# An SSD, attention and expert-retrieval block on one core: eight dense tokens fetched as gathered rows, and the v stage with v stationary

## The reference

```python
x = x + concat([y_ssd, y_diff]) @ w_out              # the mixer, 512 tokens of 1024
q  = (xb @ w_q).reshape(tb, 8, 2, 128)
sc = einsum('thjd,hjnd->thjn', q, sub_keys)          # 2 x 128 scores per head
s_half, i_half = top_k(sc, 16)
top_s, top_pos = top_k(s_half[0][:, None] + s_half[1][None, :], 16)
idx = i_half[0] * 128 + i_half[1]                    # at top_pos
g = softmax(top_s)
h = gelu(einsum('td,thkd->thk', xb, u[idx]))         # u, v: 16384 x 1024
out = einsum('thk,thkd->td', g * h, v[idx])
```

## Time and profile before

| | |
|---|---|
| median of 3 runs | 1391.71 us (1390.98 to 1391.97) |
| the profiled execution | 1390.36 us |
| its span, first to last instruction | 1388.6 us |
| granted clock of PE | 1.000 |
| PE, DVE, ACT, POOL busy | 98%, 78%, 32%, 47% of the span |
| moved by DMA | 467.69 MB, mean 337 GB/s |

### The profile page before, as it was taken

One profiled execution on the slowest core, in us unless ns is written; L12 is line 12 of the kernel. 1 busy time (PEld: TensorE's weight loads), 2 busy tenths in 40 slices (PEclk: granted clock), 3 DMA queues, 4 the chain that ended last, 5 costly groups with the idle time before them and its releaser, 6 DMA issues.

```text
span 1388.6 us, 16311 instructions
## 1 busy us (share of the span) xinstructions
PE 1364.4 (98%) x5402; PEld 934.3 (67%) x5402; DVE 1082.4 (78%) x2469; ACT 440.1 (32%) x1219; POOL 647.5 (47%) x516
## 2 busy tenths in 40 slices
PE   7999999999999999999999999999999999999999
PEld 5656648566588888888899999995444444444443
DVE  4535445899899999999998899997977677766655
ACT  2533532444412111112787887881000000000000
POOL 0000000823855443433486756774777666645430
PEclk9999999999999999999999999999999999999999
DMA  8322234975999999988799999999999999999997
GB/s 330 137 108 97 117 143 175 375 291 204 412 412 403 399 336 376 324 316 305 289 409 409 405 399 392 382 390 380 363 410 409 409 409 409 410 409 409 410 409 301
DMA packets 121763, 467.69 MB, mean 337 GB/s; under 512 B 13776, under 2 KB 14160, under 8 KB 115152
## 3 DMA queue, kind: packets, MB, share of 16 engines
q0 software_dynamic: 73728, 268.47, 49.7%
q1 hardware_dynamic: 47664, 197.66, 36.7%
q10 hardware_dynamic: 288, 0.52, 0.1%
HBM read 462.67 MB, written 3.93 MB: 336 GB/s over the span
## 4 chain that ended last, share of the span: by engine, by line
PE 71%; DVE 22%; issue 4%; ACT 1%; DMA 0%; SPq 0%; DVEq 0%; ACTq 0%
PE BANKS L953 32%; PE BANKS L929 15%; PE BANKS L729 11%; DVE X L1623 5%; PE BANKS L721 5%; PE BANKS L948 4%; DVE BIG L1434 2%; DVE BIG L1426 2%; DVE UV L1618 1%; DVE BIG L1618 1%; DVE BIG L1428 1%; DVE SMALL L1431 1%; DVE BIG L1449 1%; DVE SMALL L1423 1%; PE BANKS L701 1%
## 5 line engine op out<-in xcount | busy, mean ns | idle before, releaser
L1665 POOL DMA_INDIRECT UV<-u,IDX x173 | 217.6, 1258 | 376.6 <-DVE IDX L1495 244.4
L1665 POOL DMA_INDIRECT UV<-v,IDX x178 | 232.0, 1303 | 161.3 <-DVE X L1623 107.7
L1623 DVE SCALAR_TENSOR_TENSOR X<-UV,HG,X 128x1024 f32<-128x1024 f32 x178 | 228.4, 1283 | 33.9 <-DMA UV<-v,IDX 31.6
L1618 DVE SCALAR_TENSOR_TENSOR UV<-UV,Y 128x1024 f32<-128x1024 f32 x173 | 210.0, 1222 | 34.5 <-DMA UV<-u,IDX 34.0
L929 PE MATMUL BANKS<-T 128*128 128x256 f32 x1024 | 229.1, 379 | 0.0
L953 PE MATMUL BANKS<-T,BIG 128*128 128x512 f32 x512 | 225.2, 593 | 0.0
L953 PE MATMUL BANKS<-Y,BIG 128*128 128x512 f32 x512 | 225.1, 592 | 0.0
L929 PE MATMUL BANKS<-T,Y 128*128 128x256 f32 x992 | 221.9, 379 | 0.0
L929 PEld LDWEIGHTS BANKS<-T 128*128 128x128 f32 x1024 | 192.3, 190 | 24.5
L929 PEld LDWEIGHTS BANKS<-T,Y 128*128 128x128 f32 x992 | 186.3, 190 | 23.8
L953 PEld LDWEIGHTS BANKS<-Y,BIG 128*128 128x128 f32 x512 | 97.5, 190 | 122.3 <-issue 122.3
(11 more groups left out here) (272 smaller groups left out, 1244.7 us busy)
## 6 DMA issues: line engine op xcount, KB each, us to landing
T<-u_t SPq DMA_DIRECT2D x64, 512.0 KB, 6.7
T<-v SPq DMA_DIRECT2D x64, 512.0 KB, 6.8
Y<-v SPq DMA_DIRECT2D x64, 512.0 KB, 6.8
Y<-u_t SPq DMA_DIRECT2D x62, 512.0 KB, 6.6
BIG<-w_in SPq DMA_DIRECT2D x23, 1024.0 KB, 7.0
BIG<-w_q SPq DMA_DIRECT2D x16, 1024.0 KB, 8.9
BIG<-w_out SPq DMA_DIRECT2D x8, 1024.0 KB, 6.9
UV<-v,IDX POOLq DMA_INDIRECT x178, 9.0
```

The source lines that it names most:

```text
L1618: stt(row, row, 1.0, Y[:, n // 4, :], ALU.mult, ALU.mult, accum_out=acc).then_inc(used, 1)
L1623: stt(xb, row, HG[:, n % 2, i % UNIT:i % UNIT + 1], xb, ALU.mult, ALU.add).then_inc(used, 1)
L1665: pool.indirect_dma_start(row_place(s), None, u if kind == "ru" else v, bass.IndirectOffsetOnAxis(IDX[:, b, c:c + 1], 0)).then_inc(row_in[ ...
```

## The change

Eight of the 256 dense tokens (the first eight of block 2) are taken out of the dense part, which is now `TD` = 248 tokens wide. Their 8 x 128 = 1024 pairs of token and slot are laid out as 8 slots deep on 128 partitions (16 groups of slots by 8 tokens), so that they are done by 8 fetches of u (`mu` steps) and 8 of v (`mv`), 16 more row fetches in the same stream. Small DMAs through DRAM turn indices and weights round (`MIDX`, `MW`), ScalarE and PE copy the eight tokens to all partitions once (`my`), and `XMA` is summed back by eight small products with a selection matrix.

HBUF is 248 columns a tile, there are 62 one-hot groups in place of 64, and the v stage is turned round: pieces of v are stationary and the 248 token columns of HBUF move. The result is columns by tokens, so at the end ScalarE copies each of four banks to `OT` and PE transposes it back. `RING` goes from 8 to 7, and the buffer `YM` is new. The hand-written order of the mixer stays.

```diff
-RING = 8
+RING = 7
-NGRP = HT // NTOK
+XM = 8
+MG = P // XM
+TD = HT - XM
+NGRP = TD // NTOK
+LASTV = 3
@@ row_stream
+        m = q - LATE * UNIT - 4
+        if 0 <= m < 2 * XM and m % 2 == 0:
+            s.append(("mu", m // 2))
...
+        if 0 <= m - 2 * XM - 8 < XM:
+            s.append(("mv", m - 2 * XM - 8))
@@ work_order
-            work += [item] + rows(4 - (n >= 13))
+            work += [item] + rows(4 - (n >= 11))
...
-    work += [first] + on("sel", 0) + rows(9) + on("oh", 0) + [second] + rows(3) + on("oh", 1) + [keys, columns]
+    work += [first] + on("sel", 0) + rows(8) + on("oh", 0) + [second] + rows(3) + on("oh", 1) + [keys, columns]
...
-        while w < len(work) and spent < 3.44 * (j + 1):
+        while w < len(work) and spent < 3.35 * (j + 1):
@@ SyncE
+                if j == 46:
+                    sp.wait_ge(mi_ready, 1)
+                    sp.dma_start(m_index, MB[:, :]).then_inc(m_away, 16)
+                    sp.dma_start(m_weight, G[0:XM, HB, :]).then_inc(m_away, 16)
+                if j == 48:
+                    sp.wait_ge(m_away, 32)
+                    sp.dma_start(MIDX[:, :], m_index.rearrange("t (g k) -> g t k", k=XM)).then_inc(m_in, 16)
...
@@ TensorE, gl
-                        last = nc.tensor.matmul(PS[(i + 2) % 4][:, 0:HT], ub[:, c, :], T8[:, 1, c, :],
+                        last = nc.tensor.matmul(PS[(i + 2) % 4][:, 0:TD], ub[:, c, :], T8[:, 1, c, XM:HT],
@@ TensorE, the v stage
-                return nc.tensor.matmul(PS[4 + 2 * t + n][:, :], HBUF[:, j, t * P:(t + 1) * P],
-                                        STREAM[j % NS][:, n * HALF:(n + 1) * HALF], start=(j == 0),
-                                        stop=(j == NKEY - 1), skip_group_check=True)
+            def v_chunk(j, c):
+                at = c % 2 * HT
+                return nc.tensor.matmul(PS[4 + c // 2][:, at + XM:at + HT], STREAM[j % NS][:, c * P:(c + 1) * P],
+                                        HBUF[:, j, :], start=(j == 0 and c % 2 == 0), stop=(j == NKEY - 1), skip_group_check=True)
+            def back_to_tokens(bank):
+                pe.wait_ge(ot_done, bank + 1)
+                for c in (2 * bank, 2 * bank + 1):
+                    for b in range(HB):
+                        last = nc.tensor.transpose(PS[2 * b + c // 4][:, c % 4 * P:(c % 4 + 1) * P],
+                                                   OT[:, c, b * P:(b + 1) * P], IDENT)
+                last.then_inc(ot_full, 1)
...
+            pe.wait_ge(used, ROWSEQ[("mv", XM - 1)] + 1)
+            for c in range(KC):
+                at = c % 2 * HT
+                nc.tensor.matmul(PS[4 + c // 2][:, at:at + XM], XMA[:, c * P:(c + 1) * P], COLS[:, V_SEL:V_SEL + XM],
+                                 start=False, stop=True, skip_group_check=True)
+            for bank in range(4):
+                for c in (2 * bank, 2 * bank + 1):
+                    for j in range(NKEY - LASTV, NKEY):
+                        last = v_chunk(j, c)
+                last.then_inc(acc_full, 1)
+                if bank:
+                    back_to_tokens(bank - 1)
+            back_to_tokens(3)
@@ VectorE
+                    if step == "mu":
+                        stt(row, row, 1.0, YM[:, :], ALU.mult, ALU.mult, accum_out=MH[:, i:i + 1]).then_inc(used, 1)
+                    elif i == 0:
+                        ts(XMA[:, :], row, MHG[:, 0:1], None, ALU.mult).then_inc(used, 1)
+                    else:
+                        dve.wait_ge(used, ROWSEQ[("mv", i - 1)] + 1)
+                        stt(XMA[:, :], row, MHG[:, i:i + 1], XMA[:, :], ALU.mult, ALU.add).then_inc(used, 1)
@@ VectorE, fin
-                    for n in range(2):
-                        dve.wait_ge(acc_full, 2 * i + n + 1)
-                        xb = X[:, HB + i, n * HALF:(n + 1) * HALF]
-                        tt(xb, xb, PS[4 + 2 * i + n][:, :], ALU.add).then_inc(out_ready, 1)
+                    dve.wait_ge(ot_full, 2 * i + 2)
+                    for b in range(HB):
+                        xb = X[:, HB + b, i * HALF:(i + 1) * HALF]
+                        tt(xb, xb, PS[2 * b + i][:, :], ALU.add).then_inc(out_ready, 1)
```

More of the change, by code:

```diff
@@ L101, in work_order @@
     place = [0]
+    known = [LATE]
     def rows(m):
         out = []
-        while place[0] < len(stream) and (m or stream[place[0]][0] not in ("ru", "rv")):
+        while place[0] < len(stream) and (m or stream[place[0]][0] not in ROW_KINDS):
             item = stream[place[0]]
-            m -= item[0] in ("ru", "rv")
+            if item[0] == "ru" and item[1] >= known[0] * UNIT:
+                break
+            m -= item[0] in ROW_KINDS
             out.append(item)
@@ L225, in work_order @@
         o += rows(1 + (k % 4 == 0))
-    o += on("gm", NGRP - 1) + on("gw", NKEY - 1)
+    o += [("gm", n) for n in range(NGRP) if ("gm", n) not in o] + on("gw", NKEY - 1)
     first, second, keys, columns = pick(LATE)
@@ L428, in block_program @@
         POS = {s: i for i, s in enumerate(ORDER)}
-        rows_until = lambda step: sum(s[0] in ("ru", "rv") for s in ORDER[:POS[step]])
-        FIRST_V = rows_until(("gm", NGRP - 1))
+        rows_until = lambda step: sum(s[0] in ROW_KINDS for s in ORDER[:POS[step]])
+        FIRST_V = rows_until(("gw", NKEY - 1))
         def spaces():
@@ L971, in _ @@
-            pe.wait_ge(ge_done, NKEY)
-            pe.wait_ge(gw_done, len(WEIGHED))
-            for j in range(3, NKEY - 2):
+            for j in range(NKEY - LASTV):
+                if j == 3:
+                    pe.wait_ge(ge_done, NKEY)
+                    pe.wait_ge(gw_done, len(WEIGHED))
                 pe.wait_ge(v_in[j % NS], 16 * (j // NS + 1))
-                for t in range(HB):
-                    last = v_products(j, t)
+                for c in range(KC):
+                    last = v_chunk(j, c)
@@ L986, in _ @@
+            for j in range(NKEY - LASTV, NKEY):
+                pe.wait_ge(v_in[j % NS], 16 * (j // NS + 1))
+            for bank in range(4):
+                for c in (2 * bank, 2 * bank + 1):
+                    for j in range(NKEY - LASTV, NKEY):
+                        last = v_chunk(j, c)
+                last.then_inc(acc_full, 1)
+                if bank:
+                    back_to_tokens(bank - 1)
+            back_to_tokens(3)
         @block.scalar
@@ L1193, in _ @@
                         last = nc.scalar.activation(bank[:, 0:n], bank[:, 0:n], ACT.Gelu)
-                    if n < HT:
-                        last = nc.scalar.activation(HBUF[:, i, n:HT], bank[:, n:HT], ACT.Gelu)
+                    if n < TD:
+                        last = nc.scalar.activation(HBUF[:, i, n:TD], bank[:, n:TD], ACT.Gelu)
                     last.then_inc(ge_done, 1)
+                elif step == "my" and i == 0:
+                    nc.scalar.activation(YM[:, :].rearrange("p (c g t) -> p c g t", c=KC, g=MG),
+                                         bc(T8[:, 1, :, 0:XM], 2, MG), ACT.Copy).then_inc(my_full, 1)
+                elif step == "my":
+                    for c in range(2):
+                        act.wait_ge(my_full, c + 2)
+                        nc.scalar.activation(YM[:, c * HALF:(c + 1) * HALF], PS[5 + c][:, :], ACT.Copy).then_inc(ym_done, 1)
+                elif step == "mhg":
+                    act.wait_ge(mh_ready, 1)
+                    nc.scalar.activation(MHG[:, :], MHG[:, :], ACT.Gelu).then_inc(mhg_done, 1)
                 elif step == "gm" and JS[i] < NKEY:
@@ L1231, in _ @@
                     last.then_inc(oh_ja, 1)
+            act.wait_ge(chosen, CHOSEN[("r", 2 * PH - 1)] + 1)
+            for bank in range(4):
+                act.wait_ge(acc_full, bank + 1)
+                nc.scalar.activation(OT[:, 2 * bank:2 * bank + 2, :].rearrange("p c t -> p (c t)"), PS[4 + bank][:, :], ACT.Copy)\
+                    .then_inc(ot_done, 1)
             for n in range(2):
-                act.wait_ge(out_ready, 3 + n)
+                act.wait_ge(out_ready, HB * n + 2)
                 part = slice(n * HALF, (n + 1) * HALF)
```

110 lines of the change are left out of this document (74 added, 36 removed).

## The result

| | before | with the change |
|---|---|---|
| median | 1391.35 us (1390.98 to 1391.97) | 1399.01 us (1398.77 to 1400.64) |
| the profiled execution, its span | 1390.36, 1388.6 us | 1398.77, 1397.0 us |

The ratio is 1.0057, with a 95% interval of 1.004 to 1.0074: slower by 7.7 us. The forecast was 1403.

What follows compares the result with a forecast made beforehand. Prediction: DMA engines carrying gathered rows bound the kernel, nearly level with PE. Last row at 932.2 + 452.4 + 6.4 = 1391.0; rv, additions and store give 1399.9, 11.3 above 1388.6, so 1391.7 + 11.3 = 1403 us, range 1394 to 1411.

Steps and rivals of the forecast that it cites:

- u stage ends: End of the u stage: 945.8 us less 6.0 in its first half and 7.6 in its second, so 932.2.
- PE's end: After the v stage and the final transposes, PE alone would end near 1369.4 us.
- The rival by which PE sets it: At the kernel's end: PE decides if 185 MB pass in 433 us, 427 GB/s; 1376 us, chance 0.07.
- The rate: DMA transfers after the u stage: 409 GB/s as the ceiling when saturated, so 185.0 MB take 452.4 us.
- what would show it: Signs in the changed profile; wrong if saturated DMA exceeds 415 GB/s, rows finish before PE, or PE idles in the u stage.
- The tail: Kernel's end: the last rv steps, each behind the one before, add 2.5 us, between 0 and 3.
- theory 1: From the experiments: the bytes the DMA engines must move set when the last row is used, and with it the end.
- The hole: First choice of indices in the v stage: of 8.4 us unused transfer time, some 2 us are given back.
- The smaller ring: Row steps on VectorE: fewer ring places delay the mixer by 3 to 10 us, 1406 to 1413; chance 0.04.
- VectorE in the second half of the u stage: VectorE cannot keep up there with 7 ring places; without any gain +7.6, 1410 us; chance 0.08.
- Narrow columns: Products with narrow moving operands cost more a column, v stage 29 us more, 1403 to 1408 us; chance 0.03.
- The extra rows: Part of them hidden in better filled holes and faster running rows: 1391 to 1395 us; chance 0.06.

Runs made afterwards that it cites:

- the pair with 13 us more: Useless PE products added in the v stage: 13.0 us to the changed kernel, 1398.94 us; 12.9 us to the kernel before, 1403.91 us.
- The run with two sums and six rows less: Changed kernel, additional row every third tile in the u stage's second half, last 32 rv steps alternating between two sums: 1388.96 us, ratio 0.9983.
- the run with half of v: Changed kernel fetching only columns 0 to 511 of each v tile, all products still made: 1370.70 us, ratio 0.9853.

## Why the prediction was right, and where its numbers were off

The direction and the cause were right: the rows' bytes, not PE, decide when VectorE gets its last rows, and PE's gain is lost behind them. The sum ended 2.9 us too high (span 1399.9 forecast, 1397.0 measured). That it is no further off is partly luck, since errors of both signs cancel: the DMA engines were done 7.1 us earlier than forecast, and what follows them took 4.2 us longer. The forecast of 1403 was 4 us too high because it also added 3.1 us to the span, where these runs have 2.0.

| term of the prediction | forecast | measured |
|---|---|---|
| u stage ends | 932.2 | 932.35 |
| bytes from there to the last row | 185.0 MB | 185.9 MB |
| their time at the full rate | 452.4 us (409) | 447.0 us (416) |
| time not used in holes | 6.4 us | 4.5 us |
| DMA engines done | 1391.0 | 1383.9 |
| from there to the end of the last rv | 3.8 us | 7.2 us |
| four additions and store | 5.1 us | 5.9 us |
| PE's end | 1369.4 | 1369.5 |

The bytes are 412 x 424.15 + 409 x 26.5 + 117 x 3 of the windows above. "Measured" times of the DMA engines are worked out from these windows too.

- *PE does not set the end* held, as the pair with 13 us more shows. The rival by which PE sets it asked for 427 GB/s, and the rate was 416.
- *The rate* was the largest miss. "409 stands" took a plateau of one kernel for a limit of the engines. At 409 the same bytes would have taken 7.5 us more. The plateau was real, but 1.7% of it hung on the place of one buffer, which the change moved as a side effect. Under "what would show it" a rate above 415 was named as a sign of error, and it was one. The Trainium skill's 425 GB/s ("DMA: Bandwidth & Descriptors", section Measured) is reached by neither trace in these windows.
- *The tail* was mis-sized the other way, 7.2 us for 3.8. I let rows "land every 1.28 us" and charged VectorE 0.11 for each of 28. The 27.4 us of transfer after 1356.5 carried 11.2 MB, 21 rows, while 24 were still to be used behind the one that had just landed. Up to 15 fetches are in flight at a time, each some 29 us from issue to landing, so bytes of several later rows must have been in already; no trace shows the bytes of one fetch. VectorE then had 25 rows of 1.38 us, 34.6 us, against 27.4 of transfer. So bytes set when VectorE's last wait ended, at 1356.5; from there on the end was VectorE's chain of additions, not the DMA engines, and theory 1 is the whole account only up to there. The run with two sums and six rows less had its last row 11 us earlier, at a pitch of 1.24.
- *The hole* at the first choice: 302 GB/s from 955 to 970 us, 4.1 us unused, most of the 4.5. Of the 8.4 us unused before, some 4 were given back, not 2.
- *PE's end* was right by luck: errors cancel, as the run with half of v shows. Windows of PE with the granted clock, changed kernel:

```profile
1350.00:1354.00 4.00, 2.37 (x20) 0.89 1.02 417
1354.00:1359.00 5.00, 4.89 (x12) 0.50 1.03 419
1359.00:1362.00 3.00, 3.00 (x13) 0.85 1.03 419
```

  and of the kernel with half of v:

```profile
1350.00:1354.00 4.00, 4.00 (x29) 1.00 0.61 250
1354.00:1359.00 5.00, 5.00 (x27) 1.00 0.02 3
```

  PE waited 1.74 us for the last tile, behind the eight small products (sixteen records of 8 columns), and the granted clock then stood at 0.50, 1.2 GHz, for 5 us: 12 records of products in place of 27. Without the wait PE ended at 1364.9. The wait and the clock cost 4.6 us together, of which I had 1.6. The other way, a group of four transposes between the products cost 0.44 us, and I had 2.8 for three groups: I took their price from the earlier trace rows, whose line L912 is eight products of queries with keys, two records each, and not transposes; a transpose (L1010) is one record. And 125 tiles took 0.9 us less than forecast. None of this reached the end, since VectorE's rows were later.
- *Rivals.* The smaller ring (+1 us alone, ratio 1.0007) and VectorE in the second half of the u stage (the stage ended on time) are out. Narrow columns cost no more: the eight products of a tile take (1350.52 - 932.19)/125 = 3.347 us for 3.354 forecast. The extra rows were hidden only by the 4 us of better filled holes.

## What to carry to other kernels

When two streams end within a few microseconds of each other, work taken from the one that shows in the chain and given to the other is paid in full: here 8.4 MB of rows at 416 GB/s for a gain on PE, which then stood idle for the last 22 us of the rows, though it was still busy for 96% of the span. Give the engine in question a dozen microseconds of useless work and see whether the time moves; here that told what sets the end where the busy share did not. And before a plateau of the transfer rate goes into a sum, look at where the destination buffers lie, because a table that grows by 32 bytes ahead of them can be worth as much as the change itself.

## What the runs showed of the hardware

Transfers depend on where UV starts: 409 or 416 to 417 GB/s, in both kernels. Queues in the window from 1000 to 1350 us (packets, MB, share of the 16 engines), the changed kernel first, then with UV 32 bytes further on:

```profile
q0 software_dynamic: 24821, 90.38, 63.6%
q1 hardware_dynamic: 15083, 54.92, 38.7%
```

```profile
q0 software_dynamic: 24200, 88.12, 63.1%
q1 hardware_dynamic: 15047, 54.77, 39.3%
```

A packet of the rows' queue took 0.636 x 16 x 350 us / 24821 = 143.5 ns and then 146.0; one of the queue of the tiles, whose buffers had not moved, 143.7 and then 146.3. About half of the rows land in UV, and yet the packets of the other queue take 1.8% longer as well, so it is not only the rows in UV that are slower. Why, stays open. The Trainium skill ("DMA: Bandwidth & Descriptors", section How a descriptor splits into AXI transactions) says of reads that a descriptor which does not start on 256 bytes costs extra beats of 32 bytes for what lies ahead of it. For 4096 bytes that start 96, 128 or 160 bytes behind such a boundary, where UV's rows lie in the kernel before, the changed one and the moved one by my reckoning of the layout, an estimate by it is 131, 132 and 133 beats, an even rise. The runs show 409, 416 and 409, so by this reckoning it is not that rule. What fits is that a start 32 bytes over a multiple of 64 is slow and one on a multiple of 64 is fast. That was seen at these three starts alone, and it supposes that the first buffer starts on a multiple of 64 itself.

A VectorE sum in which each step adds to the result of the one before went at 1.38 us a step in the changed kernel, and with two sums in turn at 1.24 in the version that moves rows forward, for the same operation on 1024 columns, whose record lasts 1.28 us in both.
